# Hybrid decoder step on one core: the tail of the input projection as two column slabs of 256 and 432, with the squares and gate logits inside the query and key groups

## The reference, cut to what matters

```
z = h @ w_in                       # h: 1072 x 1024, w_in: 1024 x 2224
q_g, k_g, v_g, g_g, a_lr, c_q, c_kv, k_r = split(z)   # 256,256,512,512,16,384,256,32 columns
log_a = log_sigmoid(a_lr @ w_gate_up + b_gate) / 16   # the decays of the GLA, per key column
q   = rms_norm(c_q) @ w_uq ;  ckv = rms_norm(c_kv) ;  krope = rope(k_r)
b   = cumsum(log_a) in chunks of 64;  q_g * exp(b), k_g * exp(b_mid - b), k_g * exp(b_last - b)
```

## Time and profile before

| | before |
|---|---|
| median of 3 runs | 1519.29 us (1518.63 to 1522.09) |
| profiled execution, whole / span | 1518.05 / 1516.2 us |
| PE busy | 1452.3 us, 96% of the span, 11027 matmuls |
| PE weight load busy | 1247.6 us, 82% |
| DVE / ACT / POOL busy | 1009.3 / 667.1 / 367.9 us |
| mean granted clock of TensorE | 0.993 |

### The profile page before, as it was taken

How to read it: one execution, slowest core, us unless ns; L and a number is a source line. 1 busy time by engine, 2 the same in 40 slices (tenths; PEclk the granted TensorE clock), 3 DMA queues, 4 the chain that set the end, 5 groups by cost and what they waited for, 6 DMA issues and landing times.

```text
span 1516.2 us, 29169 instructions
## 1 busy us (share of the span) xinstructions
PE 1452.3 (96%) x11027; PEld 1247.6 (82%) x11027; DVE 1009.3 (67%) x1743; ACT 667.1 (44%) x1257; POOL 367.9 (24%) x393
## 2 busy tenths in 40 slices
PE   5999999899999999999999999999999999999995
PEld 5999998676666666567889999999999997778884
DVE  6733303866555555566678988898888894466687
ACT  2355323753566633343224555544555542435340
POOL 2101000410001024430111244444444442210006
PEclk9999999999999999999999999999999999999997
DMA  7221102110101157773223455545555548979462
GB/s 257 95 71 61 56 29 74 43 60 15 29 1 43 43 173 246 242 244 112 98 89 94 155 179 169 183 163 195 191 170 169 185 159 273 351 255 302 162 194 111
DMA packets 123141, 217.63 MB, mean 144 GB/s; under 512 B 10938, under 2 KB 69944, under 8 KB 120200
## 3 DMA queue, kind: packets, MB, share of 16 engines
q1 hardware_dynamic: 100218, 121.94, 24.9%
q0 software_dynamic: 22688, 94.38, 18.1%
q10 hardware_dynamic: 144, 0.07, 0.0%
HBM read 165.66 MB, written 50.69 MB: 143 GB/s over the span
## 4 chain that ended last, share of the span: by engine, by line
PE 83%; DVE 8%; issue 3%; ACT 3%; DMA 2%; POOL 1%; SPq 0%; DVEq 0%; ACTq 0%; POOLq 0%
PE ps L2440 9%; PE ps L2439 9%; PE ps L2438 9%; PE ps L215 7%; PE ps L217 7%; PE ps L216 7%; PE ps L1416 4%; PE ps L3100 3%; PE ps L1801 3%; PE ps L3101 3%; PE ps L3102 3%; PE ps L1453 2%; PE ps L1780 2%; PE ps L1827 2%; PE ps L1430 2%
## 5 line engine op out<-in xcount | busy, mean ns | idle before, releaser
L2438 PE MATMUL ps<-t_hi,op_hi 128*128 128x266 f32 (+1 forms) x672 | 191.6, 285 | 2.4 <-DVE gap_hi L2662 2.4
L2440 PE MATMUL ps<-t_hi,op_lo 128*128 128x266 f32 (+1 forms) x672 | 192.3, 286 | 0.0
L2439 PE MATMUL ps<-t_lo,op_hi 128*128 128x266 f32 (+1 forms) x672 | 192.1, 286 | 0.0
L2438 PE MATMUL ps<-h1T_hi,op_hi 128*128 128x266 f32 x504 | 143.5, 285 | 0.8 <-DVE gap_lo L2674 0.8
L2440 PE MATMUL ps<-h1T_hi,op_lo 128*128 128x266 f32 x504 | 144.2, 286 | 0.0
L2439 PE MATMUL ps<-h1T_lo,op_hi 128*128 128x266 f32 x504 | 143.5, 285 | 0.0
L2896 DVE TENSOR_TENSOR ring_lo<-d_raw,ring_hi 128x1024 fp32r<-128x1024 f32 x77 | 95.4, 1249 | 55.7 <-ACT ring_hi L2892 54.8
L2892 ACT ACTIVATE ring_hi<-d_raw 128x1024 fp32r<-128x1024 f32 x77 | 81.5, 1060 | 110.0 <-DMA d_raw<-t_res 58.5
L215 PE MATMUL ps<-w_hi,hT_hi 128*128 128x256 f32 (+2 forms) x448 | 126.5, 282 | 2.9 <-DVE hT_lo L338 2.9
L2438 PEld LDWEIGHTS ps<-t_hi,op_hi 128*128 128x128 f32 x672 | 126.9, 189 | 2.6 <-DVE gap_hi L2662 2.6
L2439 PEld LDWEIGHTS ps<-t_lo,op_hi 128*128 128x128 f32 x672 | 127.1, 189 | 0.0
(11 more groups left out here) (393 smaller groups left out, 3675.3 us busy)
## 6 DMA issues: line engine op xcount, KB each, us to landing
f_raw<-in_w_ffn_in SPq DMA_DIRECT2D x88, 256.0 KB, 3.3
g_res<-gap_lo SPq DMA_DIRECT2D x22, 528.0 KB, 3.6
g_mix<-in_w_down POOLq DMA_DIRECT2D x11, 1024.0 KB, 5.3
t_res<-g_mix POOLq DMA_DIRECT2D x11, 1024.0 KB, 4.2
g_mix<-g_res POOLq DMA_DIRECT2D x11, 1024.0 KB, 5.3
s_res<-g_mix POOLq DMA_DIRECT2D x11, 1024.0 KB, 4.2
d_raw<-in_w_down SPq DMA_DIRECT2D x22, 512.0 KB, 6.7
d_raw<-s_res SPq DMA_DIRECT2D x44, 256.0 KB, 3.5
```

The lines of the kernel that those rows point to most:

```text
L2438: nc.tensor.matmul(o, ah, bh, start=FIRST_IN[q] and k == 0, stop=False, skip_group_check=again)
L2439: nc.tensor.matmul(o, ah, bl, start=False, stop=False, skip_group_check=again)
L2440: last = nc.tensor.matmul(o, al, bh, start=False, stop=k == 3, skip_group_check=again)
```

## The change: two tail slabs instead of three, and other places for the side jobs

The 688 tail columns were slabs of 230, 230 and 228; they become 256 and 432. With one slab fewer there are 66 groups: 0 to 17 are the tail, 18 to 23 q, 24 to 29 k, 30 to 47 v and 48 to 65 g. The wide slab has buffers of its own, which overlap others, so some addresses, load conditions (`W_AFTER`) and small tiles move. In the first loop `w_lo` of slab 1 is made after the second row tile is normalised and no longer before.

The side jobs get new numbers: `gate_logits` after groups 20 to 25 on PE, their copies after 21 to 26 on ACT, `log_gate` after 24 and 27, `decays` after 29, and the squares two tiles at a time after groups 18 to 22. Counted from q's first group, `gate_logits` begins after the third q group where it began ahead of the first, and the second `log_gate` comes after k's fourth group where it came after k's first.

```diff
+        a_low = [at(f"a_low{i}", [ROWS0, n], o) for i, (n, o) in enumerate(((256, 6464), (432, O_QG), (256, 7488)))]
+        w_raw.append(at("w_raw_wide", [P, KC, 432], O_RING + 16384))
+        w_lo.append(at("w_lo_wide", [P, KC, 432], O_RING + 16384, F32R))
+        w_hi.append(at("w_hi_wide", [P, KC, 432], O_RING + 30208, F32R))
...
-        SLABS = [("t", W_TAIL, 230), ("t", W_TAIL + 230, 230), ("t", W_TAIL + 460, 228),
-                 ("q", W_Q, 256), ("k", W_K, 256), ("v", W_V, 256), ("v", W_V + 256, 256),
-                 ("g", W_G, 256), ("g", W_G + 256, 256)]
+        SLABS = [("t", W_TAIL, 256), ("t", W_TAIL + 256, 432), ("q", W_Q, 256), ("k", W_K, 256),
+                 ("v", W_V, 256), ("v", W_V + 256, 256), ("g", W_G, 256), ("g", W_G + 256, 256)]
+        W_AFTER = (None, None, None, 0, 1, 3, 4, 5)
...
-                if j in (1, 6):
-                    w_lo_dve(dve, {1: 1, 6: 2}[j])
+                if j == 6:
+                    w_lo_dve(dve, 2)
...
                 norm_scale(j, n, xs[j % XS][0:n, :]).then_inc(h_ready, 1)
+                if j == 1:
+                    w_lo_dve(dve, 1)
...
             offsets(dve)
-            w_lo_dve(dve, 5)
+            w_lo_dve(dve, 4)
             products(dve)
-            add_low(dve, 3)
+            add_low(dve, 2)
...
                 mm_group(pe, g)
-                if g == 20:
+                if g == 18:
                     turn_rank(pe, 0)
                     turn_rank(pe, 1)
-                elif g == 22:
+                elif g == 19:
                     turn_rank(pe, 2)
-                elif 26 <= g < 32:
-                    gate_logits(pe, g - 26)
+                elif 20 <= g < 26:
+                    gate_logits(pe, g - 20)
...
-            HIGH_AFTER = {19: 3, 20: 4, 34: 5, 40: 6, 49: 7, 58: 8}
+            HIGH_AFTER = {20: 3, 25: 4, 31: 5, 40: 6, 49: 7}
+            SQUARES_AFTER = {18: (1, 2), 19: (3, 4), 20: (5,), 21: (6, 7), 22: (8, 0)}
...
-                if groups[g][0] == S_TAIL:
-                    squares_of(groups[g][1], g)
+                for i in SQUARES_AFTER.get(g, ()):
+                    squares_of(i)
...
-                elif 27 <= g < 33:
-                    logit_out(act, g - 27)
-                if g == 30:
+                if 21 <= g < 27:
+                    logit_out(act, g - 21)
+                if g == 24:
                     log_gate(act, 0)
-                elif g == 33:
+                elif g == 27:
                     log_gate(act, 1)
-                elif g == 36:
+                elif g == 29:
                     decays(act)
```

More of the change, by code:

```diff
@@ L137, in build @@
         hT_both = at("hT_both", [P, KC, LOW_ROW + ROWS0], 9536, F32R)
-        a_low = [at(f"a_low{i}", [ROWS0, 256], 6464 + 1024 * i) for i in range(2)]
+        a_low = [at(f"a_low{i}", [ROWS0, n], o) for i, (n, o) in enumerate(((256, 6464), (432, O_QG), (256, 7488)))]
+        A_LOW = (0, 1, 2, 0, 2, 0)
         W_AT = (O_RING, O_RING + 16384, O_V + 2048)
@@ L252, in load_w @@
         def load_w(sp, s):
-            if s > S_TAIL:
-                sp.wait_ge(group_done, last_group[W_SLOT.index(W_SLOT[s]) if W_TURN[s] == 1 else s - 2] + 1)
+            if W_AFTER[s] is not None:
+                sp.wait_ge(group_done, last_group[W_AFTER[s]] + 1)
             _, c, n = SLABS[s]
             sp.dma_start(w_raw[W_SLOT[s]][:, :, 0:n],
-                         ins["w_in"][:, c:c + n].rearrange("(k p) n -> p k n", p=P)).then_inc(w_loaded[W_SLOT[s]], 16)
+                         ins["w_in"][:, c:c + n].rearrange("(k p) n -> p k n", p=P)).then_inc(w_loaded[W_SEM[s]], 16)
         def w_hi_act(act, s):
             n, slot = SLABS[s][2], W_SLOT[s]
-            act.wait_ge(w_loaded[slot], 16 * (W_TURN[s] + 1))
+            act.wait_ge(w_loaded[W_SEM[s]], 16 * (W_TURN[s] + 1))
             nc.scalar.activation(w_hi[slot][:, :, 0:n], w_raw[slot][:, :, 0:n], ACT.Copy).then_inc(w_hi_done, 1)
@@ L291, in sp_ab @@
                 load_x(sp, i)
-            for s in (3, 4):
-                load_w(sp, s)
+            load_w(sp, 3)
             sp.wait_ge(h_ready, NT)
@@ L298, in sp_ab @@
             sp.dma_start(scanm[:, :], ins["c_scan"]).then_inc(gla_loaded, 16)
-            for s in range(5, len(SLABS)):
+            for s in range(4, len(SLABS)):
                 load_w(sp, s)
@@ L394, in dve_ab @@
             offsets(dve)
-            w_lo_dve(dve, 5)
+            w_lo_dve(dve, 4)
             products(dve)
-            add_low(dve, 3)
-            for s in (6, 7, 8):
+            add_low(dve, 2)
+            for s in (5, 6, 7):
                 w_lo_dve(dve, s)
@@ L584, in out_group @@
                     j = short_groups.index(g)
-                    nc.scalar.activation(a_low[j % 2][:, 0:n], ps[LOW_ROW:LOW_ROW + ROWS0, bank, 0:n], ACT.Copy).then_inc(low_kept, 1)
+                    nc.scalar.activation(a_low[A_LOW[j]][:, 0:n], ps[LOW_ROW:LOW_ROW + ROWS0, bank, 0:n], ACT.Copy).then_inc(low_kept, 1)
                     act.wait_ge(low_added, j + 1)
@@ L597, in out_group, with squares_of @@
                 nc.scalar.activation(dst, src, ACT.Silu if kind == "g" else ACT.Copy).then_inc(group_out, 1)
-            def squares_of(i, g):
-                act.wait_ge(group_out, g + 1)
+            def squares_of(i):
+                act.wait_ge(group_out, last_group[S_TAIL] + 1)
                 act.wait_ge(h_ready, NT)
@@ L695, in build @@
         t_e = at("t_e", [P, 2, T], O_GATE + 8576)
-        lane = at("lane", [P, 1], O_DECAY)
-        ptab = at("ptab", [2 * DEC_B, 16], O_DECAY + 64, I32)
-        pagef = at("pagef", [2 * DEC_B, 16, 8], O_DECAY + 128)
+        lane = at("lane", [P, 1], O_QG + 8192)
+        ptab = at("ptab", [2 * DEC_B, 16], O_QG + 8192 + 64, I32)
+        pagef = at("pagef", [2 * DEC_B, 16, 8], O_QG + 8192 + 128)
         row_at = at("row_at", [P, 2 * DEC_B, 4], 3520, I32)
```

23 lines of the change are left out of this document (11 added, 12 removed).

## The result

| | before | after |
|---|---|---|
| median of 4 runs each | 1519.18 us (1518.63 to 1522.09) | 1532.11 us (1531.25 to 1535.36) |
| ratio after / before | | 1.0078, 95% interval 1.0066 to 1.0089 |
| profiled execution, whole / span | 1518.05 / 1516.2 us | 1532.04 / 1530.2 us |
| matmuls on PE | 11027 | 10819 |
| mean granted clock of TensorE | 0.993 | 0.988 |

The change makes the kernel slower, as forecast, but by about 12 to 13 us and not by 8.1. The time lies 1.1 us above the range.

What follows compares the result with a forecast made beforehand. PE was taken as the bound (83% of the chain of waits). The terms -4.7 + 0.7 + 1.0 - 0.7 + 10.1 + 1.7 = +8.1 us, on 1519.29, gave 1527.4 us, range 1524 to 1531.

Steps and rivals of the forecast that it cites:

- PE's start: At the front, the first slab has 256 columns instead of 230, so PE starts later: +0.7 us.
- the wait near 56 us: Inside the projection, PE's wait of 0.69 us at 56.15 goes because DVE is never late again: -0.7 us.
- All that lies ahead of slab v: From the start to the q slab, PE gets 3.7 us ahead in work done.
- The wait at slab v: At slab v's first matmul, PE waits for DVE's low part behind the second gate logarithm's chain: +10.1 us.
- The +1.0 us at the second tile: At the front, PE loses its gap before the transposes but waits 2.9 us for the wide low part: net +1.0 us.
- the 15.2 us: At slab v, DVE's time from low part to first group's copy, 15.2 us, against PE's 16: the six banks last.
- The clock behind that wait: After the slab v wait, PE runs 3.6 us at 213 instead of 112 ns per matmul: +1.7 us.
- There is one restart of PE at the lower clock here before and after, so it cancels.: At the front, the restart at the lower clock occurs in both kernels, so no term was added.
- Against the profiled execution ... +8.1: Over the whole kernel, the terms sum to +8.1 us on the profiled execution, giving 1526.2 us.
- the give-back: Rival: stages after slab v return half of the 10 us wait, about 1522 us; chance 0.07.
- Proportional columns: Rival: tail matmuls cost by their columns, so two slabs save nothing over three: 1532.1 us; chance 0.03.
- ACT never lagged: Rival, in the q groups: ACT falls behind with the squares and PE waits for logits, up to 3 us, 1530; chance 0.05.

Runs made afterwards that it cites:

- e2: The changed kernel with 60 matmuls of unused result ahead of slab v's first group, filling PE's wait: 1527.28 us, ratio 1.0057.
- e3: The kernel before with three and a half repeated scans on DVE ahead of `offsets`, so PE waits at slab v: 1528.63 us, ratio 1.0057.
- e4: The kernel before, unchanged, profiled a second time: 1526.35 us in one execution.
- e6: The changed kernel with ranks, logits, squares, logarithms and decays earlier, and slab v's low part ahead of `offsets`: 1520.14 us, ratio 1.0004 to before.
- e8: The kernel before, unchanged, profiled a third time: 1515.83 us in one execution.
- e7: The kernel of e6 with 20 matmuls of overwritten result in the wait for the wide low part: 1518.93 us, ratio 0.9989 to before.
- e9: The changed kernel, unchanged, profiled a third time: 1532.37 us in one execution.
- e5: The changed kernel, unchanged, profiled a second time: 1531.37 us in one execution.
- e10: The kernel of e7 with two more fills of unused results, at 258 us and in the down projection: 1518.15 us, ratio 0.9981 to before.
- e11: The changed kernel with only 16 additional matmuls in the wait at the start of the down projection: 1533.37 us, ratio 1.0079 to before.
- e1: The changed kernel with slab v's low part made between DVE's two cumulate steps instead of behind `offsets`: 1525.64 us, ratio 1.0044 to before.

## Why the prediction was wrong

The direction, the place and the mechanism were right, and these steps of the sum came out as put:
- PE's start: +0.75 us for +0.7. The wide low part took 3.75 us for 3.79, the wait for it 2.46 for 2.9, and it is the only one left there; the wait near 56 us is gone.
- 432 columns every 194.4 ns for 193.9, and 208 matmuls fewer. All that lies ahead of slab v came to -3.5 us (three profiles: -3.36 to -3.61) for -3.7.
- The wait at slab v: 10.04 us for 10.1.

Two of these came out on readings that hold only in part. The +1.0 us at the second tile stood on POOL's two steps getting shorter, with a tile up to 2 us earlier; they took 1.31 + 0.57 us for 1.93 + 1.46, and the tile was ready 0.77 us earlier. That PE came to the transposes without a gap is also because its first group ran every 213 ns until 21.4 us. And the 15.2 us "from the low part to the copy of slab v's first group" include the 5.27 us in which DVE waited for ACT ahead of `products`; in the changed kernel it is 9.8 us (159.88 to 169.68). The conclusion, that the six banks last behind the waiting PE, was right, with more room than counted.

Three things did not come out as put:
- **The clock behind that wait** was sized 1.7 us and cost 2.1 to 2.3 (2.3 is the growth of the shift behind it, 2.1 the difference to e2; 20 distances of 213.5 ns from 160.35 to 164.62, where 117.3 would do, make 1.9 of it). I took the length of the low stretch from the one restart that I had. With half a microsecond of small differences, the shift at the attention stage is 9.14 and not 8.1 us.
- **"There is one restart of PE at the lower clock here before and after, so it cancels."** It doesn't. I read it off a single profile, in which the old kernel happened to have it; it has it in one profile of four (with e3), and the new front in six of seven. Over the three profiles of each kernel the difference at 262.63 is 9.16 + 1.15 = 10.3 us.
- **"Against the profiled execution ... +8.1"**, that is, that everything behind slab v follows one for one. Between 262 and 1268 us it does on average (9.9 us there), although single profiles differ by 5 us. In the down projection the changed kernel then loses 2.1 us more: its mean shift at 1312 us is 13.8, that of before 1.85. This is the unsettled part, and it may be chance, since the old kernel has the same loss of 4.1 us there in e4.

The sum over these: 8.1 + 1.1 (clock and small losses) + 1.1 (front) - 0.4 (between) + 2.1 (down projection) = 12.0, and the mean whole times of three profiles, 1531.93 and 1520.08, are 11.85 apart, which is also what the ratio 1.0078 gives.

Of the rivals, the give-back went the other way: later stages took more instead of returning some. Proportional columns would have given the number 1532.1, which is the measured one by chance, and are refuted by 194.4 ns. ACT never lagged. That the forecast's own range ended at 1531.0 had this reason: it had a term for the clock behind my new wait only, and none for the other places (22, 261, 376 us and the down projection), each of which costs 1.5 to 4.1 us in some executions. The bounds of its own terms, simply added, reach +13.5 us, 1532.8; the text doesn't say how they became 1531.

The two slabs as such are near neutral (e6). What made the kernel slower is that only two groups of k are left, instead of five, between ACT's second logarithm and slab v, so that a chain of 17.7 us on ACT and DVE no longer fits.

## What to carry to other kernels

When work is taken out of the bounding engine, or side jobs get other places in its list, list what ran in its shadow, with the slack of each chain to its next use; a chain safe by 1.7 us before is the new bound as soon as more than that is taken from its cover, and here the new places alone took 11.8 us. And move such a chain as a whole: with only its first consumer moved, the next (here `add_low` behind full PSUM banks) took half of the gain back. Before a sum of a few us is built on one profile, profile the kernel two or three times, since a restart that "cancels" may be there only once.

## What the runs showed of the hardware

- The lower TensorE clock (1.2 GHz, granted clock 0.50) followed short waits too, but not each time. At 22 us in the old front: low after 1.86 us (first profile of before), not after 1.75 (e4), 1.02 (e8) and 0.92 (e3). After the wait of 1.6 to 2.0 us at 259 to 272 us: low in e4, e6 and e7, not in the other nine where it wasn't filled. After the wait of 2.4 us at 841 to 855 us: low in six of the thirteen profiles (after and e9 among them), not in before, e4, e8, e3, e5, e6 or e10. Near 300 us, where PE waits 1.0 to 1.3 us three times within 7 us: low in ten of thirteen. After 3 us and more it was low in all cases seen (seven at the down projection, six around slab v), apart from the next point.
- PE's first group at 16 us ran at one matmul of 230 columns every 213 ns until 19.1 us and at 112 from 19.5 us on in before, and at one of 256 columns every 213 ns until 21.4 us in after, although the granted clock of these stretches is given as 1.00. The distances there say more than that column.
- One later restart costs 1.2 to 2.9 us beside the wait itself. With matmuls of useless results in the wait it wasn't seen: in five places of four kernels (slab v in e2, the front in e7 and e10, 258 us in e10, the down projection in e11) the clock stayed at 1.00. Each is a single profile, and only around slab v (six of six) and at the down projection after 3 us and more (seven of seven) was it always low without them.
- The places may hang together, on few profiles. In e4 and e7 the clock fell at about 260 us, stayed at 1.00 near 300 us, where it fell in ten of the eleven other profiles, and fell again at 376 us, where it did in no other; no wait of PE stands in the 8 us ahead of that in either. In e6 it fell at 261 and at 299 us and not at 376. What released it isn't known.
- The first transfers of the down projection, same sizes and same order of issue, took between 5.1 us (e7) and 8.7 us (e1) from issue to first use; within one kernel 5.4 to 8.2 us (before, three executions).
